# Four feed-forward stages start on x times the norm's weights, and apply the token factor and the shift behind PSUM

## What is computed

```python
def rmsnorm(x, g):
    y = x32 * lax.rsqrt(jnp.mean(x32 * x32, axis=-1, keepdims=True) + RMS_EPS)
    return y.astype(x.dtype) * g
def modulate(z, g, shift, scale):
    return rmsnorm(z, g) * (1.0 + scale) + shift
def swiglu(h, wi, wo):
    a, u = jnp.split(h @ wi, 2, axis=-1)
    return (jax.nn.silu(a) * u) @ wo
...
x = x + 0.5 * m[8] * swiglu(modulate(x, norm_g[l, 2], m[6], m[7]), ffn2_wi[l], ffn2_wo[l])
```

## Time and profile before

| what | value |
|---|---|
| median of 3 runs | 3236.94 us (3234.47 to 3237.37) |
| the profiled execution's own time | 3234.64 us |
| its span in the trace | 3232.1 us |
| TensorE busy | 3152.3 us, 98% of the span |
| VectorE, ScalarE busy | 1860.3 us (58%), 1026.0 us (32%) |
| granted TensorE clock, mean | 0.986 |

### The profile page before, as it was taken

The page is one execution under the profiler, slowest core; times in us unless marked ns, Lnnn a source line. Parts: engine busy times, 40 slices in busy tenths (PEclk is TensorE's granted clock), DMA queues, the critical chain, the costliest instruction groups (busy, mean ns, idle before and its releaser), DMA issues.

```text
span 3232.1 us, 37291 instructions
## 1 busy us (share of the span) xinstructions
PE 3152.3 (98%) x15190; PEld 2528.8 (78%) x15190; DVE 1860.3 (58%) x2673; ACT 1026.0 (32%) x1480; POOL 10.2 (0%) x23
## 2 busy tenths in 40 slices
PE   8999999998899999999999999999999998899998
PEld 7888888776678888788877888788887764578887
DVE  7876555645555554666646554566665655554444
ACT  4212222345442222322234222332224344332222
POOL 0000000000000000000000000000000000000000
PEclk9999999999999999999999999999999999899999
DMA  6433432210034433255522443235551210123331
GB/s 229 140 118 124 149 125 85 66 44 11 1 124 152 154 124 117 85 207 190 197 92 79 169 144 131 79 118 206 190 178 62 76 55 1 56 91 102 97 98 52
DMA packets 101846, 365.03 MB, mean 113 GB/s; under 512 B 11247, under 2 KB 12543, under 8 KB 101421
## 3 DMA queue, kind: packets, MB, share of 16 engines
q1 hardware_dynamic: 100636, 357.94, 32.4%
q0 software_dynamic: 1040, 4.71, 0.4%
HBM read 360.51 MB, written 2.10 MB: 112 GB/s over the span
## 4 chain that ended last, share of the span: by engine, by line
PE 89%; DVE 6%; ACT 3%; issue 1%; DMA 1%; SPq 0%; POOL 0%; DVEq 0%; ACTq 0%; POOLq 0%
PE ps L192 25%; PE ps L194 25%; PE ps L193 25%; PE ps L196 4%; PE ps L197 2%; DVE SQ L610 1%; PE ps L496 1%; DVE HL L599 1%; DVE WL L184 1%; PE ps L2373 1%; ACT WH L179 1%; PE ps L2606 0%; DVE XT L855 0%; DVE RAW L1317 0%; PE ps L2706 0%
## 5 line engine op out<-in xcount | busy, mean ns | idle before, releaser
L192 PE MATMUL ps<-HH,WH 128*128 128x512 f32 x2464 | 973.8, 395 | 4.2 <-ACT S L769 2.2
L194 PE MATMUL ps<-HH,WL 128*128 128x512 f32 x2464 | 960.9, 390 | 0.0
L193 PE MATMUL ps<-HL,WH 128*128 128x512 f32 x2464 | 960.0, 390 | 0.0
L179 ACT ACTIVATE WH<-RAW 128x1024 fp32r<-128x1024 f32 x456 | 459.1, 1047 | 622.4 <-PE ps L194 366.5
L184 DVE TENSOR_TENSOR WL<-RAW,WH 128x1024 fp32r<-128x1024 f32 x456 | 542.9, 1219 | 92.3 <-ACT WH L179 92.1
L192 PEld LDWEIGHTS ps<-HH,WH 128*128 128x128 f32 x2464 | 462.9, 188 | 116.7 <-issue 9.9
L194 PEld LDWEIGHTS ps<-HH,WL 128*128 128x128 f32 x2464 | 462.7, 188 | 98.7
L193 PEld LDWEIGHTS ps<-HL,WH 128*128 128x128 f32 x2464 | 463.1, 188 | 97.1 <-issue 4.6
L855 DVE SCALAR_TENSOR_TENSOR XT<-ps,DER,XT 128x512 f32<-128x512 f32 x512 | 346.4, 682 | 249.0 <-PE ps L194 234.2
L192 PE MATMUL ps<-GH,WH 128*128 128x512 f32 x1056 | 412.5, 391 | 4.8 <-DVE GL L793 4.8
L194 PE MATMUL ps<-GH,WL 128*128 128x512 f32 x1056 | 411.1, 389 | 0.0
(11 more groups left out here) (356 smaller groups left out, 2467.8 us busy)
## 6 DMA issues: line engine op xcount, KB each, us to landing
RAW<-in_w_modt SPq DMA_DIRECT2D x200, 512.0 KB, 5.0
RAW<-in_ffn_wi SPq DMA_DIRECT2D x176, 512.0 KB, 4.8
RAW<-in_ffn_wo SPq DMA_DIRECT2D x88, 512.0 KB, 4.9
RAW<-in_w_gu SPq DMA_DIRECT2D x88, 512.0 KB, 4.3
RAW<-in_w_in SPq DMA_DIRECT2D x44, 512.0 KB, 3.6
RAW<-in_w_down SPq DMA_DIRECT2D x44, 512.0 KB, 4.2
RAW<-in_w_out SPq DMA_DIRECT2D x16, 512.0 KB, 4.4
STG<-in_w_modt SPq DMA_DIRECT2D x10, 512.0 KB, 12.8
```

The source lines that it names most:

```text
L179: act.e.activation(u.hi, u.ld.view, ACT.Copy).then_inc(u.hi_done.sem, 1)
L192: pe.e.matmul(out, wh, x[0], start=first, stop=False)
L193: pe.e.matmul(out, wh, x[1], start=False, stop=False)
L194: m = pe.e.matmul(out, wl, x[0], start=False, stop=last)
```

## The change

In the four stages the first chunk no longer multiplies the normed and shifted data. It multiplies U, which is x times the norm's weights (`AheadSplit`: `UH` on ScalarE, L681 of the new file; `UL` on VectorE, L686). U needs no token factor, so it is made piece by piece inside the last down projection or output projection before the stage. The squares are summed fully on VectorE (`Sums(full=True)`, two more additions), one product by ones gives the sums on all partitions at once (`Factor.sum`, L705, placed in chunk 0 behind k=2), and `Newton` then works on 128x512 tiles where it had 6x128. Behind PSUM, chunk 0 is multiplied by the factor (L925), and the shift's contribution, one number per hidden feature, is added as a bias in silu (L899) and in the product (L930). That number is the shift times the weights, summed over the 1024 features: `BiasDot` on VectorE (eight instructions on 128x256), `BiasSum` (L756, two products of one column) and `BiasCopy`. It needs the chunk's two weight tiles unsplit, so they are loaded a second time. The other 21 chunks use the normed data as before; `NormSplit` stays and reads the factor from SBUF. The `Busy` steps at these four places go. The list's order changes too: chunk 1's weight split, `Factor`, `NormSplit` and `Up(0)` are now added ahead of the lines on `Diag` quoted above.

```diff
@@ class AheadSplit, Factor (new)
+    def scalar(self, act):
+        P, k = self.P, self.k
+        act.wait_ge(*self.ready)
+        act.wait_ge(*self.gain)
+        act.e.activation(P.UH[:, k, :], P.XT[:, k, 0:T], ACT.Identity, scale=P.mod_a(self.mi, k)).then_inc(self.hi.sem, 1)
+    def vector(self, dve):
+        P, k = self.P, self.k
+        dve.wait_ge(*self.hi)
+        dve.e.scalar_tensor_tensor(P.UL[:, k, :], P.XT[:, k, 0:T], P.mod_a(self.mi, k), P.UH[:, k, :].bitcast(F32),
+                                   ALU.mult, ALU.subtract).then_inc(self.lo.sem, 1)
...
+    def sum(self, pe):
+        P = self.P
+        pe.wait_ge(*self.total)
+        pe.wait_ge(*self.bankfree)
+        pe.e.matmul(P.banks[7], P.ONE, P.SA[:, 0:T], start=True, stop=True).then_inc(self.summed.sem, 1)
...
@@ class BiasDot (new), vector; BiasSum, tensor
+        for k in range(8):
+            w, b = self.view[:, :, k * 128:(k + 1) * 128], P.mod_b(self.mi, k)
+            if k == 0:
+                dve.e.tensor_scalar(P.ACC, w, b, None, ALU.mult).then_inc(self.part[k].sem, 1)
+            else:
+                dve.wait_ge(*self.part[k - 1])
+                dve.e.scalar_tensor_tensor(P.ACC, w, b, P.ACC, ALU.mult, ALU.add).then_inc(self.part[k].sem, 1)
...
+        pe.wait_ge(*dot.part[7])
+        for i, q in enumerate(dot.order):
+            m = pe.e.matmul(P.banks[self.bank][:, 508 + q:509 + q], P.ACC[:, i, :], P.ONE[:, 0:1], start=True, stop=True,
...
@@ class Up, scalar and vector
+                if q == 0 and self.factor:
+                    act.wait_ge(*self.scaled[q])
+                    act.wait_ge(*self.biased)
+                    act.e.activation(s, s, ACT.Silu, bias=P.BIAS[:, q:q + 1]).then_inc(self.silu[n].sem, 1)
+                    continue
...
+                    dve.e.tensor_tensor(d, out, self.factor.R, ALU.mult).then_inc(self.scaled[q].sem, 1)
+                    if q:
...
+                        dve.e.scalar_tensor_tensor(s, d, P.BIAS[:, q:q + 1], s, ALU.add, ALU.mult).then_inc(self.mul[n].sem, 1)
+                        dve.wait_ge(*self.hi[n])
+                        dve.e.tensor_tensor(gl, s, gh.bitcast(F32), ALU.subtract).then_inc(self.lo[n].sem, 1)
...
@@ def ffn
-            F = Ffn(self, ctx, mi, segs, self.norm_split(ctx, mi, segs, after, ready=bool(early)))
+            if ahead:
...
+                units, self.units = self.units, self.split([wi[1], wi[NF + 1]])
+                F.factor = self.add(Factor(self, R))
+                self.add(NormSplit(self, mi, segs, F.h, after, R=R))
+                self.add(Up(F, 0, units))
...
@@ def ffn, run of a Down
                     for d in range(8):
                         self.add(DownPart(down, d))
+                        if nxt is not None and last and d:
+                            self.add(AheadSplit(self, nxt, d - 1, down.evac[d - 1, 0][0]))
                         if d in (1, 3, 5):
                             split_ahead()
+                        if dot and fs == tail[0] and d == 5:
+                            bias["dot"] = self.add(BiasDot(self, dot[0], bias["lds"]))
+                        if dot and fs == tail[1] and d in (2, 4):
+                            self.add((BiasSum if d == 2 else BiasCopy)(bias["dot"]))
+                    if nxt is not None and last:
+                        self.add(SumsEnd(sums))
+                        self.add(AheadSplit(self, nxt, 7, down.evac[7, 0][0]))
...
@@ def out_products, run of a job
+                if d:
+                    self.add(AheadSplit(self, nxt, d - 1, evac[d - 1]))
+                if d == 2:
+                    bias["lds"] = self.bias_loads(wi)
+                elif d == 4:
+                    bias["dot"] = self.add(BiasDot(self, nxt, bias["lds"]))
+                elif d == 5:
+                    self.add(BiasSum(bias["dot"]))
+                elif d == 6:
+                    self.add(BiasCopy(bias["dot"]))
...
@@ def mixer_pool, adding
+                    if k:
+                        self.add(AheadSplit(self, mi + 1, k - 1, adds[k - 1].evac))
...
```

More of the change, by code:

```diff
@@ L408, in late @@
     def late(self, dve, k):
-        if 1 < k < 7:
+        if 1 < k < (9 if self.full else 7):
             P, w, j = self.P, self.w, k - 1
@@ L562, with __init__ @@
 class NormSplit(Step):
-    def __init__(self, P, mi, segs, h, after, ks=range(8)):
+    def __init__(self, P, mi, segs, h, after, ks=range(8), R=None):
         self.P, self.mi, self.segs, self.h, self.after = P, mi, segs, h, after
+        self.R = [R] if R is not None else [P.banks[4], P.banks[5]]
         self.rstd = P.rstd
@@ new lines, with __init__, scalar, vector @@
+class Factor(Step):
+    def __init__(self, P, R):
+        self.P, self.R, self.total = P, R, P.total
+        self.summed = P.safree = P.s["rs_sum"].next()
+        self.newton = Newton(P, self.summed)
+        P.rstd = P.sqfree[0] = self.done = self.newton.done
+        self.bankfree = P.biased
+    def sum(self, pe):
[3 more added lines that the diff above has]
+        pe.e.matmul(P.banks[7], P.ONE, P.SA[:, 0:T], start=True, stop=True).then_inc(self.summed.sem, 1)
+    def scalar(self, act):
+        P = self.P
+        self.newton.scalar(act, self.R, P.banks[7], 1024, P.EPSC)
+    def vector(self, dve):
+        P = self.P
+        self.newton.vector(dve, self.R, P.SQ[:, 0, 0:T], P.banks[7], 1024)
@@ new lines, with __init__, vector @@
+class BiasDot(Step):
+    def __init__(self, P, mi, lds):
+        self.P, self.mi, self.lds = P, mi, lds
+        self.before, self.shift = P.biased, P.modt[mi, 0]
+        self.part = [P.s["bias_dve"].next() for _ in range(8)]
+        self.summed = P.s["bias_mm"].next()
+        for ld in lds:
+            ld.users = [self.part[7]]
+        at = [ld.slot for ld in lds]
+        lo, step = min(at), abs(at[0] - at[1])
+        self.view = P.RAW[:, lo:lo + step + 1:step, :]
+        self.order = [at.index(lo), 1 - at.index(lo)]
+    def vector(self, dve):
+        P = self.P
+        for ld in self.lds:
+            dve.wait_ge(*ld.landed)
+        dve.wait_ge(*self.before)
+        dve.wait_ge(*self.shift)
+        for k in range(8):
[5 more added lines that the diff above has]
+                dve.e.scalar_tensor_tensor(P.ACC, w, b, P.ACC, ALU.mult, ALU.add).then_inc(self.part[k].sem, 1)
@@ new lines, with __init__, tensor, scalar @@
+class BiasSum(Step):
+    def __init__(self, dot, bank=7):
+        self.dot, self.bank = dot, bank
+    def tensor(self, pe):
+        P, dot = self.dot.P, self.dot
+        pe.wait_ge(*dot.part[7])
+        for i, q in enumerate(dot.order):
+            m = pe.e.matmul(P.banks[self.bank][:, 508 + q:509 + q], P.ACC[:, i, :], P.ONE[:, 0:1], start=True, stop=True,
+                            skip_group_check=True)
+        m.then_inc(dot.summed.sem, 1)
+class BiasCopy(Step):
+    def __init__(self, dot, bank=7):
+        self.dot, self.bank = dot, bank
+        dot.P.biased = self.done = dot.P.s["bias_act"].next()
+    def scalar(self, act):
+        P = self.dot.P
+        act.wait_ge(*self.dot.summed)
+        act.e.activation(P.BIAS, P.banks[self.bank][:, 508:510], ACT.Copy).then_inc(self.done.sem, 1)
@@ L683, in __init__ @@
         self.F, self.c, self.units = F, c, units
+        self.factor, self.biased, self.h = F.factor if c == 0 else None, P.biased, F.h
+        if self.factor:
+            self.h = H(P.UH, P.UL, None)
+            self.h.hi, self.h.lo = dict(P.ahead.hi), dict(P.ahead.lo)
+        self.scaled = {}
         ns = len(F.segs)
@@ L738, in tensor @@
                         products(q, n, k)
+                    if self.factor and k == 2:
+                        self.factor.sum(pe)
         else:
@@ L3043, in norm_split, with bias_loads, ffn @@
         return h
-    def ffn(self, mi, segs, wi, wo, after, following, blk=None, rows=(), early=()):
+    def bias_loads(self, w):
+        return [self.add(LoadStep(Load(self, src))).ld for src in (w[0], w[NF])]
+    def ffn(self, mi, segs, wi, wo, after, following, blk=None, rows=(), early=(), ahead=False, nxt=None, dot=None):
         with self.scope() as ctx:
@@ L3072, in ffn @@
             for c in range(NF):
-                jobs.append(up(c))
+                if c or not ahead:
+                    jobs.append(up(c))
                 if c < 2:
@@ L3167, in mixer_pool @@
             self.rstd_of(T // 128)
-            sums = Sums(self, T)
-            zfree, ztile, bfree, prods, copies, means = {}, {}, {}, {}, {}, {}
+            sums = Sums(self, T, True)
+            zfree, ztile, bfree, prods, copies, means, adds = {}, {}, {}, {}, {}, {}, {}
             def prod(g):
@@ L3200, in mixer_pool @@
             mean(3)
-            self.add(Busy(self, 4))
             last = add(3)
+            self.add(SumsEnd(sums))
+            self.add(AheadSplit(self, mi + 1, 7, last.evac))
         return [last.evac]
```

99 lines of the change are left out of this document (76 added, 23 removed).

## The result

The changed kernel takes 3286.72 us (median of 4 runs, 3285.07 to 3287.45), the kernel before in the same comparison 3237.15 (3234.47 to 3237.73). The ratio is 1.0157, 95% interval 1.0145 to 1.0169: slower by about 50 us.

A forecast was written before the change was run, and what follows sets the result against it. TensorE, 98% busy, was taken as the bound. Stage losses 15.4 + 14.4 + 9.9 + 0, clock 7.2 and BiasSum 0.8 make 47.7 us; on 3234.64 that is 3282.3, plus 2.3 for the median: 3284, range 3263 to 3300.

The forecast's parts named there:

- Entries close: At the four stage entries the gap before chunk 0 goes and chunk 0 runs without pause: 8.5 and 0.6 us each.
- the chain from N to it is 20.1 us: Before chunk 1 in three stages, TensorE's spreading product waits for VectorE's diagonal and starts 20.1 us after N.
- N: The time at which VectorE starts the Newton step at a stage's entry.
- Rival 1: At the entries, the diagonal's wait does not hold TensorE, only the norm does: 3247 us, chance 0.04.
- N of the second and third stage: Rounds of 2.8 us before these stages put Newton's start at 1321.0 and 1726.4; spreading product 15.4 and 14.4 us later.
- N of the first and fourth stage: Behind the output projections, Newton starts at 944.3 and 2859.1, with 1.4 us waiting for the bias chain and 0.4 for products.
- Fourth stage, no change: The fourth stage has no spreading product; the 8.5 us won at its entry go again in waiting for the norm.
- The clock, 2.4 us at each of three waits: After three idle stretches of 15 us TensorE's clock is lower: 2.4 us each, 7.2 in all, bounds 0 and 10.5.
- Stages in sum: Spreading product later by 9.9, 15.4 and 14.4 us in stages one to three, none in the fourth, plus clock and BiasSum.
- The wait for the full sum, 5 us or so: In the second and third stage TensorE waits about 5 us at the full sum (L705).
- Rival 2: Faster: entries close, 36 us, less 3.4 for full sums and 3.6 for bias: -29, 3208 us, chance 0.03.
- Rival 3: Extra loads delay chunk 0's weights at two or three entries, or a weight split, 5 to 8 us each: 3300+, chance 0.10.

The follow-up runs named there:

- run 1: Changed kernel with VectorE making the diagonal ahead of the Newton step in the three stages that spread the condition vector: 3246.77 us (ratio 1.0030).
- run 3: Changed kernel with BiasSum and BiasCopy a round later in the two output projections: 3285.54 us (ratio 1.0150).
- run 4: Changed kernel with ScalarE making the high part of U of a piece ahead of the next piece's square: 3265.49 us (ratio 1.0089).
- run 6: Changed kernel with VectorE's eight-instruction bias chain cut in two, four in round 3 and four in round 4 of the output projections: 3281.13 us (ratio 1.0138).
- run 2: Changed kernel with the diagonal between the norm and the evacuation of chunk 0, its place in the kernel before: 3267.17 us (ratio 1.0093).
- run 9: run 8 with chunk 2's weights split ahead of the rest of chunk 0's evacuation and the second spreading product behind chunk 2's products: 3211.87 us (ratio 0.9925).
- run 8: Changed kernel with the edits of run 1, run 4 and run 6 together, plus chunk 1's products in chunk 0's order: 3233.69 us (ratio 0.9994).
- run 5: Changed kernel with 28 dummy products ahead of the first spreading product in the three stages that have one: 3280.57 us (ratio 1.0137).

## Why the prediction was right

The forecast was 3284 with 3263 to 3300, the result 3286.7. By its own steps:

- **Entries close.** Yes, to 0.9 us at the first and fourth stage and without a gap at the two others.
- **TensorE is held by the spreading product, the chain from N to it is 20.1 us.** Measured 20.31, 20.26 and 20.33. Run 1 shows that this one wait is 40 us with its clock (38 between the profiled executions). Rival 1, that the norm alone holds, needed products to pass a waiting one; none did. Its 3247 is what run 1 measured once the diagonal was out of the way (3246.8), though by other parts: the first and fourth stage lost 2 us each there by the bias, where the rival had nothing, and the second 0.8 and the third 0.8 less than it said. The Trainium skill, "TensorE: Matmul & The Clock Gate", in the table at its head, names weight loads alone as pulled ahead; the trace agrees, for 13 to 15 us chunk 1's products stood behind L261, though in the first stage VectorE and ScalarE had the norm's first piece ready at 950.6, ahead of chunk 0's end at 951.4. The same table calls VectorE's and ScalarE's queues strictly first in, first out; runs 3 and 4 agree, each with a wait that followed the order alone.
- **N of the second and third stage.** On the clock of before, 1320.7 and 1725.8, predicted 1321.0 and 1726.4. A round was 2.72 us, predicted 2.8.
- **N of the first and fourth stage.** 946.5 and 2861.5, predicted 944.3 and 2859.1: 2.2 and 2.4 us late. The term that was mis-sized is the bias chain: "a wait of 1.4 us, and 0.4 for the two small products". The wait was 1.38 us, as sized, but it stood for more. Piece 5 was 2.33 us late and not 1.8, as the low part of the weights behind the chain held TensorE for another 0.57 us. Then the clock fell, which the sum had at nothing (0.50, 0.50 and 0.69 in the 1-us stretches from 926 to 929): 1.3 and 1.6 us, by comparison with run 4 and with the two executions in which it did not fall. The rest, 1.2 us at pieces 6 and 7 against 0.7 predicted, stayed in run 6. Measured 4.85 and 5.10 us in all, of which halving the chain gave back 2.9 and 3.2. That I put the wait down to `BiasSum` was wrong as to the cause, as run 3 shows.
- **Fourth stage, no change.** The entry gave back 2.35 us and the mixer ahead lost 5.10; a loss of 2.75 by the bias, 2.15 up to chunk 2. It is N's own lateness of 2.4 that shows here, so that the norm holds this entry, as predicted, is right. The wait there was for the norm's high part (L595, 5 times 0.5 us), not its low part as I had written.
- **The clock, 2.4 us at each of three waits.** 1.66, 2.11 and 2.17, together 5.9 against 7.2; the 2.9 us of the two output projections come on top. The price is not a fixed one: in run 2 it was 1.9 to 2.9 us behind waits of 8 to 10 us.
- **Stages in sum.** 13.95, 17.4, 16.2 and 2.15 us, predicted 12.3, 18.2, 17.2 and 0 (the 0.8 us of `BiasSum` shared between the second and third). The first and fourth are 1.7 and 2.2 over, by the bias, the two others 0.8 and 1.0 under. Of the other 1.4 us most lies in a mixer that the change leaves alone; the 0.47 us behind the second stage's entry are `BiasSum` in its last down projection. The total is nearer than its parts, which is luck: the errors of the stages, 3.8 us up and 1.8 down, partly cancel, and the medians lie 49.6 us apart where the spans lie 51.2.
- **The wait for the full sum, 5 us or so.** 5.82 in the second stage, 2.77 in the third, little more than half of that.
- **Rival 2, faster,** said the chain must fit under chunk 0. It can't, but run 9 shows that it needn't: with the chain out of TensorE's way and the three moves of runs 8 and 9, the kernel is 25 us faster than before. **Rival 3, late loads:** SP did wait for the bias chain in front of the loads of chunk 0, 18.4 us long, until 924.6, in the first mixer. But TensorE waited no more than 0.51 us before 938.81 for chunk 0's weights, and it waited for ScalarE's split of them, two copies that ran from 936.40 without idle time in front. So the weights were there, and the loads held nothing.
- **Small slips of the sums.** 1341.1 less 1325.63 is 15.5, not 15.4, and 8 us with 7 down and 3 up around 3284 is 3269 to 3295, not 3266 to 3296. The row of 2728 to 2730 shows the second half of an idle time of 2.90 us, which ended at 2730.07. None of these changes the forecast.

## What to carry over

When work is taken from in front of a stage, look in every engine's order for what used to be hidden by it, down to the small instructions: here three diagonals of 1.2 us each on VectorE, left behind the norm and an evacuation, cost 40 us, because the product that reads them stood ahead of a whole chunk. A wait named after one reader may belong to the place of the work on its engine: moving the reader changed only the name here (run 3), moving half of the work took away 3 of 5 us (run 6). And two engines that hand pieces to and fro should each do the older piece first, or a round becomes the sum of both (2.72 against 1.92 us in run 4).

## What the runs showed of the hardware

- Short waits can bring the clock down, and the same waits don't always do it. After 1.38 and 0.57 us of idle time with four one-column products between them it was at the lower level for some 3 us (0.60, 0.50, 0.50, 0.69 for 925 to 929), and likewise after 1.90 and 1.17 us in run 8. But in the fourth stage of run 2, and of run 5, the same two waits left it at 1.00 throughout:

```profile
2872.00 0.60 PE L756 MATMUL ps<-K,ACC 128*128 128x1 f32 x4 [1.38 <-DVE ACC L743]
...
2871.00:2885.00 14.00, 11.91 (x53) 9.65 (x54) 8.88 (x12) 6.88 (x10) 0.00 (x0) 1.00 0.61 225
```

  Piece 7 was 3.5 us late there, against 5.1 in the same stage of the changed kernel and of runs 1 and 3, so the fall costs 1.6 us. What decides between the two is open. Two waits of 0.58 us at the same place (run 4) left the clock at 1.00, and so did a wait of 0.5 us every 1.45 us in run 1 (952 to 960).
- The mixer ahead of the fourth stage, which no edit touches, took between 2.0 us less and 3.5 us more than in the profile of before in these ten profiled executions. The pooling mixer, from its first to its last untouched square, varied by 2.9 us (0.1 less to 2.8 more). What moves them stays open. Where single runs are compared by a few microseconds, that part has to be taken out by stages, as above.
